# Two layers of a hybrid encoder, written out one by one instead of looped on the engines

## The reference

```
for l in range(DEPTH):
    h = rms_norm(x, attn_norm_g[l])
    proj = h @ w_in[l]
    ya = banded_attention(qa, ka, va, 128, a_sink[l]) @ w_branch_a[l]
    yb = mixture of three dilated_attention(qg, kg, vg) @ w_branch_b[l]
    merged = sigmoid(parts[-2]) * ya + sigmoid(parts[-1]) * yb
    x = x + merged @ w_out[l]
    x = x + hier_moe(rms_norm(x, ffn_norm_g[l]), ...)   # 32 experts, 2 of them per token
return rms_norm(x, final_norm_g)
```

## Time and profile before

| | us |
|---|---|
| median of 3 runs | 1419.51 |
| lowest and highest | 1416.78, 1419.99 |
| the profiled execution's own time | 1414.65 |
| its span in the trace | 1413.0 |
| PE busy | 1241.5 |
| DVE busy | 592.0 |
| ACT busy | 398.2 |

### The profile page before, as it was taken

How to read it: one execution, slowest core, us unless ns; L and a number is a source line. 1 busy time by engine, 2 the same in 40 slices (tenths; PEclk the granted TensorE clock), 3 DMA queues, 4 the chain that set the end, 5 groups by cost and what they waited for, 6 DMA issues and landing times.

```text
span 1413.0 us, 18694 instructions
## 1 busy us (share of the span) xinstructions
PE 1241.5 (88%) x6416; PEld 813.5 (58%) x6417; DVE 592.0 (42%) x1395; ACT 398.2 (28%) x731; POOL 240.0 (17%) x183
## 2 busy tenths in 40 slices
PE   5999988999997998887489999889999979978881
PEld 5877766788884433332177777667888734423330
DVE  4467676233344222221254677753333432322115
ACT  5334335333231110000153444444332300100003
POOL 0314140022101111111003233201220011111100
PEclk9999999999999999998899999999999989999996
DMA  5432220463544899999433222106437539999975
GB/s 185 127 96 84 76 90 2 149 218 108 205 183 186 367 424 424 424 424 417 162 122 116 90 91 90 45 16 223 164 104 283 217 123 424 423 423 425 424 333 199
DMA packets 59486, 306.76 MB, mean 217 GB/s; under 512 B 11376, under 2 KB 11376, under 8 KB 45056
## 3 DMA queue, kind: packets, MB, share of 16 engines
q1 hardware_dynamic: 48256, 281.57, 51.3%
q0 software_dynamic: 10992, 23.25, 4.4%
q10 hardware_dynamic: 144, 0.76, 0.1%
HBM read 290.33 MB, written 23.07 MB: 222 GB/s over the span
## 4 chain that ended last, share of the span: by engine, by line
PE 61%; DMA 21%; DVE 7%; issue 4%; ACT 3%; DVEq 3%; SPq 0%; ACTq 0%; POOL 0%; POOLq 0%
DMA gu<-in_gu_w 17%; PE bank L431 13%; PE bank L433 13%; PE bank L432 13%; PE bank L681 10%; PE bank L694 4%; PE bank L566 2%; DVEq L1062 1%; DMA h_rows<-xn 1%; ACT prob L850 1%; PE bank L502 1%; DVE prob L1085 1%; PE bank L675 1%; PE bank L533 1%; DMA yld<-y_rows 1%
## 5 line engine op out<-in xcount | busy, mean ns | idle before, releaser
L681 PE MATMUL bank<-gu,xgt 128*64 128x512 f32 x1024 | 245.9, 636 | 49.8 <-DMA gu<-in_gu_w 46.8
L431 PE MATMUL bank<-h_hi,w_hi 128*128 128x512 f32 x640 | 253.4, 396 | 6.1 <-DVE h_lo L1022 3.6
L433 PE MATMUL bank<-h_hi,w_lo 128*128 128x512 f32 x640 | 249.5, 390 | 0.0
L432 PE MATMUL bank<-h_lo,w_hi 128*128 128x512 f32 x640 | 249.1, 389 | 0.0
L980 DVE TENSOR_TENSOR w_lo<-raw,w_hi 128x1024 fp32r<-128x1024 f32 x112 | 139.2, 1243 | 185.2 <-ACT w_hi L779 184.3
L681 PEld LDWEIGHTS bank<-gu,xgt 128*64 128x64 f32 x1024 | 79.1, 146 | 213.1 <-issue 168.5
L779 ACT ACTIVATE w_hi<-raw 128x1024 fp32r<-128x1024 f32 x112 | 118.1, 1055 | 101.2 <-PE bank L433 101.2
L431 PEld LDWEIGHTS bank<-h_hi,w_hi 128*128 128x128 f32 x640 | 120.2, 188 | 32.4 <-DVE h_lo L1022 4.0
L433 PEld LDWEIGHTS bank<-h_hi,w_lo 128*128 128x128 f32 x640 | 120.1, 188 | 25.5
L432 PEld LDWEIGHTS bank<-h_lo,w_hi 128*128 128x128 f32 x640 | 120.3, 188 | 23.7
L694 PE MATMUL bank<-dn,zt 128*64 128x512 f32 x512 | 116.9, 598 | 6.2 <-ACT zt L939 3.3
(11 more groups left out here) (181 smaller groups left out, 1627.2 us busy)
## 6 DMA issues: line engine op xcount, KB each, us to landing
gu<-in_gu_w SPq DMA_DIRECT2D x28, 4096.0 KB, 37.6
raw<-in_stream SPq DMA_DIRECT2D x112, 512.0 KB, 3.4
dn<-in_dn_w SPq DMA_DIRECT2D x28, 2048.0 KB, 36.6
gu<-in_gu_w SPq DMA_DIRECT2D x32, 512.0 KB, 5.5
swp<-pj SPq DMA_DIRECT2D x136, 64.0 KB, 2.0
dn<-in_dn_w SPq DMA_DIRECT2D x16, 512.0 KB, 5.7
yld<-y_rows SPq DMA_DIRECT2D x16, 512.0 KB, 7.1
h_rows<-xn POOLq DMA_DIRECT2D x8, 512.0 KB, 10.5
```

What stands on the lines that cost most here:

```text
L431: mm(dst, ah, bh, start=start, stop=False)
L432: mm(dst, ah, bl, start=False, stop=False)
L433: return mm(dst, al, bh, start=False, stop=stop)
L681: last = mm(bank[b][e * CAP:(e + 1) * CAP, :], xgt[:, x_s, k, e * CAP:(e + 1) * CAP], gu[w_s][:, e, k, :], start=k == 0, stop=k == KD - 1)
```

## The change

The loop over the layers becomes a loop of the builder. Each engine's program then holds both layers one after the other; `l` is a whole number while the program is built, so what was computed in registers from it is a constant. The inner loops over gates and extra rounds stay as they are. Nothing else is touched.

```diff
--- before.py
+++ after.py
@@ -366,7 +366,7 @@
-            with sp.Fori(0, L) as l:
+            for l in range(L):
                 for i in range(NT):
                     if 4 <= i < NQ + 4:
                         swap_halves(l, i - 4)
@@ -448,7 +448,7 @@
             pe.sem_inc(pv_ok, ahead[pv_ok])
             pe.wait_ge(cst_ld, 16)
-            with pe.Fori(0, L) as l:
+            for l in range(L):
 
                 for t in range(TT):
                     pe.wait_ge(xn_ok, l * TT + t + 1)
@@ -804,7 +804,7 @@
             norm(0)
-            with act.Fori(0, L) as l:
+            for l in range(L):
                 square(TT - 1, l)
                 scale_x(TT - 2, l)
                 root(TT - 1, 2 * l * TT + TT - 1)
@@ -1012,7 +1012,7 @@
             masks_in()
             v.drain()
-            with dve.Fori(0, L) as l:
+            for l in range(L):
                 mean(TT - 1, 2 * l * TT + TT - 1)
                 rstd(slice(TT - 1, TT), 2 * l * TT + TT - 1).then_inc(rs_ok, 1)
                 split_lo(l, 0)
@@ -1357,7 +1357,7 @@
             pool.sem_inc(mlo_ok, ahead[mlo_ok] + 1)
-            with pool.Fori(0, L) as l:
+            for l in range(L):
 
                 pool.wait_ge(x_ok, l * TT + 1)
```

## The result

| | before | after |
|---|---|---|
| median of 6 runs each, side by side | 1419.65 us | 1410.77 us |
| lowest and highest | 1416.78, 1420.40 | 1409.56, 1412.96 |
| the profiled execution's own time | 1414.65 us | 1411.42 us |

The ratio is 0.9943 (95% interval 0.9930 to 0.9956), so the change saves 8.9 us between the medians. Over the three the mean ratio is 0.9955, a gain of 6.4 us; I explain 6.4, not 8.9.

A forecast was written before the change was run, and what follows sets the result against it. TensorE was seen as the main limit, latency deciding between layers. Terms 1.1 + 0.2 + 0.4 + 0.2 + 0.3 = 2.2 us, off the 1419.51 us median, gave 1417.3 us, range 1412.5 to 1421.0.

The forecast's parts named there:

- The seam: Between the layers: without ACT's and DVE's jump back, the second layer's first matmul comes 1.1 us earlier; ends 0.9 and 1.7.
- if PE set no limit: Between the layers: upper end of the back-edge term, 1.7 us, the amount by which ACT and DVE get earlier.
- The other engines' jumps are hidden: Between the layers: PE, GpSimd and SP jump while waiting or ahead of need, so removing their jumps gains 0.
- early weight tiles collide with the y rows: Between the layers: SP's weight loads start up to 6 us earlier while y rows land; 1420.1 us at most, chance 0.07.
- Loop entry: Start of layer 0: DVE's 0.27 us gap before its first loop operation falls to 0.07, gaining 0.2 us.
- Routing's casts: Routing: two casts into rounds_i lose their computed place, 0.11 us each in two layers, gaining 0.4 us.
- everything else: Attention and other routing waits: register steps the trace doesn't separate; 0.3 us taken, low end 0, high end 3.8.
- My sign for the register case: Attention: PE's idle time falling by over 1 us a layer would show that exposed register steps matter.
- The register steps matter: Rival, attention: late sequencers hurt the chain over three engines, so removing register steps gains more; 5.7 us, 1413.8 us, chance 0.27.
- The inner loops: Rival, gates: shifted code makes back edges stall for fetches, about 2.6 us each, six times; 1425.1 us half covered, chance 0.08.
- The flat price for a branch: Skill page: 51 ns a branch, 108 compare-and-branch; by it the layers' back edge costs nothing, whole gain 1.1 us.
- the fetch rule: Skill page: a taken branch out of the fetched window stalls for a fetch; that price goes with the jump.

The follow-up runs named there:

- the three: Three side-by-side comparisons of the unchanged kernel and the whole change: ratios 0.9943, 0.9959 and 0.9963.
- filled: Filling matmuls added in attention's idle time: to the kernel before 1424.34 us, to the written-out one with layer registers 1420.19, to the changed one 1418.17.
- cut: GpSimd's part of the rotation cut to 64 of 512 columns, other values computed: kernel before 1405.89 us (0.9923), changed kernel 1399.57 us (0.9876).
- The kernel with registers kept: Against the kernel before, both layers written out on all engines, the layer's number still in a register: 1414.68 us, ratio 0.9967.
- the hinted kernel: The kernel before with its layer loops and registers kept, plus a hint at the loops' back edge: 1417.28 us, ratio 0.9983.
- the second comparison: The whole change run again against the kernel before, beside the kernels with only some engines written out: 1410.96 us, ratio 0.9959.
- the third: The whole change run a third time against the kernel before, beside the kernels with filling matmuls: 1413.96 us, ratio 0.9963.

## Why the prediction was wrong

**The seam, 1.1 forecast, 2.5 measured.** In the two traces of before it has 31.85 and 31.5 us, in the three of after 29.3, 29.0 and 29.1. With the filled and the cut kernels taken in, the averages are 32.2 us for four with all loops and 29.1 for eleven with none, 3.0 us; the filled and the cut one with loops are the longest of all (32.9 and 32.4). My term failed at two places.

- **PE's queue behind x was taken from one trace as if it were fixed.** The path was right: PE still set the limit, for in after the fillers hold the weight loads until 713.28 + 1.64 = 714.92, and tile 3's transposes start there. But they start 4.7 us after x is ready (714.85 - 710.18), in before 6.3 (718.81 - 712.47): 1.7 us sooner, where I had 0.9. I had taken the fillers after tile 1 at their place of before, 1.28 us behind x (713.75); in after they start 0.61 behind x. In the 4.8 us around it TensorE's granted clock is 0.54 on average in before and 0.68 in after, and tile 1's transposes take 1.46 and 1.04 us. The kernel with registers kept, in which the clock rises as late as in before (0.55, transposes 1.39 us), has what my sum described. Its last piece of x, its fillers after tile 1 and its first matmul:

```profile
711.44 1.28 DVE L1334 SCALAR_TENSOR_TENSOR x<-yld,rt,x 128x1024 f32<-128x1024 f32 x1
...
713.93 1.64 PEld L447 LDWEIGHTS bank<-cst 128*128 128x128 f32 x14
...
720.70 0.50 PE L431 MATMUL bank<-h_hi,w_hi 128*128 128x512 f32 x1 [1.63 <-DVE h_lo L1022]
```

  From x ready to the first matmul it has 720.70 - 712.72 = 7.98 us, 1.2 less than before's 9.21. The other ten written-out traces have 7.5 to 7.8. That the measured 1.7 equals my end "if PE set no limit" is chance.
- **"The other engines' jumps are hidden" was wrong for PE.** PE itself waits long, but with its jump, 3.33 us, the y rows are ready 0.9 us later for everyone. I had looked at each engine's own idle time, not at what its fetch does to others.

In the two traces I compare, 1.7 + 0.85 = 2.55 us.

The rival "early weight tiles collide with the y rows" was right in its start (SP's first load at 698.23, behind the last y row by 0.1 us) and cost nothing, as given.

**Loop entry, 0.2 forecast.** DVE's gap went from 0.27 to 0.08 us, as foretold:

```profile
17.96 0.29 DVE L964 CAST mask_b<-mask_f 128x256 bf16<-128x256 f32 x1
18.33 0.15 DVE L986 TENSOR_SCALAR small<-small 128x1 f32<-128x1 f32 x1
```

Layer 0's first matmul starts at 24.8 us on average in the eleven traces without loops, at 25.4 in the four with them: 0.6 us. Single traces of either kind lie between 24.2 and 26.0, so this is no sharp number, and what brings more than 0.2 is open.

**Routing's casts, 0.4 forecast.** The gaps are 0.07 us, as foretold for the chain of the earlier trace rows:

```profile
441.31 0.16 DVE L1278 CAST rounds_i<-small 1x2 int32<-1x2 f32 x1
441.54 0.16 DVE L1280 SCALAR_TENSOR_TENSOR small<-small 128x1 f32<-128x1 f32 x1
441.77 0.14 DVE L1282 CAST rounds_i<-small 1x1 int32<-1x1 f32 x1
```

The stage around them varies by more than 0.2 us from trace to trace, so whether the end moved with them can't be read.

**Register steps, the term "everything else", 0.3 forecast.** This is the term that was mis-sized. All register steps together are worth 1.7 us by one pair of kernels (registers kept against the change, 0.9967 and 0.9955), 2.0 or 3.8 by the filled pair (medians or ratios), and 4.0 by the hinted kernel; I had 0.4 + 0.2 + 0.3 = 0.9. So the term was too small, by how much isn't known. Nor is it known where the steps cost. My sign for the register case, PE idling over 1 us less in each layer's attention, didn't come: PE idles there for 13.6 and 13.7 us in before and for 14.3 and 14.8 in after. The low end may hold as I argued it, or the clock and the collisions cover the gain.

**The sum and its base.** The seam's 2.5, the start's 0.6 and 1.7 to 4.0 for the registers make 4.8 to 7.1 us, around the 6.4 measured; only the seam is pinned to rows, so about half of the gain has no place in the trace. The first comparison with its 8.9 us fell outside the range by the mis-sized terms and by luck: the same kernel had 1410.96 us in the second comparison, outside too, and 1413.96 in the third, within the range. I had gone by the spread of three runs, 3.2 us; 122 runs of before spread over 10 us.

**The rivals.** "The register steps matter" had the nearest number, 1413.8 us, for a reason that holds in part at most: it had 4.6 us for them (0.2 + 0.4 + 0.2 + 3.8), and the runs leave 1.7 to 4.0, none of it found in attention. The inner loops didn't meet a block's edge: their branches still take 45 ns, and the gates of layer 0 are as full as before, with 139.30 of 140 us. The flat price for a branch, weighed against the first term, needs a correction: the row that I set beside it, ACT's 45 ns at L884, is a compare-and-branch, for which the same section gives 108 ns and not 51, so at the inner loops the trace is below the page rather than in agreement with it. The flat price missed the outer edge by a factor of over 20; the fetch rule beside it was the right one to follow.

## What to carry to other kernels

A jump to code that has to be fetched cost 2.5 to 3.3 us here on ACT, DVE and PE, and it is to be counted where the engines jump at a point of latency. Look at where each stall lies in the chain: those of ACT and DVE stood behind x, that of PE ahead of it, and their prices added up. Ask of a stall that lies hidden on its own engine what it does to others, as with PE's fetch and the scatter. A hint at the back edge brings the seam's gain (29.5 us against 31.7) while the code stays short; in the time it showed 2.4 us, not clear of no change. Writing the layers out brought 6.4. And a profile is one execution: before a stage's difference of 1 to 2 us is explained, look at the same stage in a second run of the same kernel.

## What I hadn't expected of the hardware

- GpSimd's elementwise work in attention stretches DVE operations by 23 us a layer: DVE is busy for 150.4 to 151.8 us with it and for 128.4 without. Cutting that work down to an eighth took 11 to 12 us off either kernel, nearly twice what the change brings. The cut also shortens GpSimd's own work (56 us busy in layer 1's attention of before, 17.5 with the cut), and no run parts this from the stretched operations.
- TensorE's clock fell at the end of attention behind 1 to 3 us of idle time in 16 of the 17 traces without fillers, and keeping it up with filling matmuls (0.959 against 0.954) made both kernels 4 to 5 us slower; six fillers take 1.6 us, and the gaps they went into are mostly 1.1 to 1.6.
- Written-out code for two layers was fetched in 28 packets (q14) against 44 for the loop. With the register steps kept it took 38, so most of the difference is the instructions that are gone.
